# An encoder layer on one core: filter pieces every two and a half attention steps instead of three, and the scores' sum and maximum in one instruction

## The chip, the core and the metric

The kernel is written in Bass for one core of one Trainium2 chip. A core has five engines, each with its own in-order queue: TensorE (PE), VectorE (DVE), ScalarE (ACT), GpSimd (POOL) and SyncE (SP), which here only issues DMAs. They meet through semaphores. The metric is device microseconds of one execution.

## What is computed

One bidirectional encoder layer over a prompt of 1024 tokens and a sample of 512 tokens, 1024 channels wide. Three dilated window attentions (groups of 8 heads), two long convolutions (done as DFTs), gates, an output projection and two RMS norms. The part that the change touches is the attention, and a preparation of the convolution's filters that runs beside it. Cut to what matters, one attention group is:

```
logits = einsum(q, k) * hd ** -0.5 + bias
logits = where(valid, logits, -1e30)
m = max(logits, axis=-1)
p = exp(logits - m)
den = sum(p, axis=-1)
o = einsum(p, v) / den ;  lse = m + log(den)
```

The three groups are then mixed by a softmax over their `lse`.

## The kernel before, in words

**Stages.** First come normalisation and the convolution's input projection (to about 568 us), then attention (to about 1328 us), then the convolutions by DFT (to about 1930 us), then the gates, the branch products and the output.

**Attention steps.** Attention runs in 6 half groups `H` (4 heads each) of 24 steps: 144 steps `N` (`NSTEP`). A step is one pair of heads on one tile of 128 tokens. PE's loop over N does, in this order: in odd steps the scores of the next two steps (`score_pair`, L1423); the transposes of this step's probabilities (`turn`, L1436); the product with the values of the step before (`value`, L1451); and a share of the projections q, k and v of the next half group (`project`, L1290, through `PARTS`). The last half group has no next one. So from step 120 to step 137 each step has only two or three small parts of its own late value tiles (12 or 18 matmuls of 256 columns), and steps 138 to 143 have none.

For step N+1, DVE (`scored`) adds the bias to the scores out of PSUM (L2172) and takes the negated maximum (L2178). ACT's loop over N does `copy` (the transposed probabilities out of PSUM, L1774), `evacuate` (a projection, L1755), `prob` of step N+1 (two exponentials, each with a sum that is read out after it, L1766), `result` in odd steps (L1783, L1784), and then its share of a filter piece. A step's `turn` waits for its `prob`, and the next `prob` stands behind `copy` on ACT: this loop between PE and ACT is the shortest period that a step can have.

**Filter pieces.** 48 pieces (`NPIECE`) of the filters' taps are loaded (`load_piece`, L980), combined on DVE (`piece_first`, `piece_second`, L2192 to L2201), split into a high and a low fp16 half (`piece_hi` on ACT, L1795; `piece_low` on DVE, L2207; two of each per piece) and stored (`store_piece`, L988 and L990). `piece_at(slot, lag)` says in which slot a piece's parts stand: slot 13 + N is attention step N, and the parts of a piece stand 1, 2, 3 and 4 slots behind its start. There is one buffer `py` for the first half of a piece, so `piece_hi(p, 0)` waits until the first store of piece p-1 has landed:

```
if p >= 1:
    act.wait_ge(py_out, 16 * p)
```

**SP's queue** runs over the same slots: stores and the next load of the pieces, then, by their slot, four bulk loads for the DFT stage: `itab` (L1025), the first signal (L1003) and the two halves of the first filter slab (L1037). When all projections are done it loads the DFT tables and two more slabs (L1053, L1049, L1055, L1043).

Of the kernel before, what the change touches and what calls it, by code (L numbers as in the profile page):

```python
# [21 lines left out]
ALU = mybir.AluOpType  # L22
ACT = mybir.ActivationFunctionType
AX = mybir.AxisListType
F32, FP16, I32 = mybir.dt.float32, mybir.dt.float16, mybir.dt.int32

P = 128
# [15 lines left out]
NEG = -1e30  # L43
# [220 lines left out]
def build(nc, ins, cst, y_p, y_s):  # L264
# [9 lines left out]
    with ExitStack() as ctx:  # L274
# [5 lines left out]
        ps = ctx.enter_context(nc.psum_tensor("ps", [P, 8, BANK], F32))  # L280
# [83 lines left out]
        lg = [grid(2, 2 * P) for _ in range(2)]  # L364
        pr = [grid(2, 2 * P) for _ in range(2)]
# [4 lines left out]
        stat = [cols[:, 2 * HH * i:2 * HH * i + 2 * HH] for i in range(6)]  # L370
# [56 lines left out]
        def hg16(a, n):  # L427
# [23 lines left out]
        names = """ld_small ld_tabs ld_gain dve_steps ld_w0 ld_w1 w_amax w_all w_scale w_hi w_lo g_amax g_all  # L451
            root_seed g_scale rows_T cols_ok fcols_ok pads_ok n_sq n_mean n_root n_rstd n_scaled n_T n_evA n_evD
            hn_saved u_ready u_evac u_mid u_tap u_conv h_mm h_arg h_sin b_mm b_rows b_stored b_copied a_ready a_evac
            a_score a_biased a_max a_prob a_pT a_ptcopied a_ov a_oevac f_gen f_gen_used f_ge f_up f_pq f_maxed f_alled ld_bound ld_ke ld_ko ld_ftab16
            p_first p_hi p_lo f_r f_im f_y f_post
            ld_hx ld_ftab ld_itab g_cmb g_third g_sc g_exp m_mul b_maxed b_alled b_scaled b_hi b_lo h_hi h_lo m_acc o_sq o_root o_r o_y""".split()
        S = {n: sem(n) for n in names}
# [33 lines left out]
        STEPS = NT * 2  # L491
# [154 lines left out]
        NPIECE = len(PIECES)  # L646
        PRELUDE, PIECE0 = NQK + 1, 5
# [8 lines left out]
        def piece_part(p, z, h):  # L656

            words = py if z == 0 else px_half(p, 1)
            return words.bitcast(FP16)[:, 4 * FQ * h:4 * FQ * (h + 1)]

        def piece_at(slot, lag):

            n = slot - PIECE0 - lag
            return range(n // 3, n // 3 + 1) if n % 3 == 0 and 0 <= n < 3 * NPIECE else range(0)

        def spectra(i, p, h):

# [10 lines left out]
        def wait_ready(eng, u):  # L678
            eng.wait_ge(bank_ready[u[0]], u[1] + 1)
# [232 lines left out]
        def _(sp):  # L912
# [100 lines left out]
            for slot in range(PRELUDE + NSTEP):  # L1013
# [17 lines left out]
                for part_ in range(2):  # L1031
                    if slot == TAIL + 6 + 3 * part_:
# [3 lines left out]
                        c = slice(8 * FQ * part_, 8 * FQ * part_ + 8 * FQ)  # L1036
                        sp.dma_start(first_ke_words[:, c], ks_d[0, 0][:, c]).then_inc(S["ld_ke"], 16)  # L1037

            def load_ke(i):
                pieces_stored(PIECE_END[i])  # L1040
                if i >= 2:
                    wait_ready(sp, uk[i - 1][K0_UNITS - 1])
                sp.dma_start(ke_words, ks_d[i, 0]).then_inc(S["ld_ke"], 16)  # L1043

            def load_ko(i):
# [14 lines left out]
            for i in range(NI):  # L1060
                s, q, o = ITEMS[i]
# [6 lines left out]
                c0, nch = chans(i)  # L1068
# [28 lines left out]
        def _(pool):  # L1097
# [63 lines left out]
            def load_bias(H):  # L1161
                g, h0 = H // 2, HH * (H % 2)
                if H >= 2:
                    pool.wait_ge(S["a_biased"], STEPS * (H - 1))
                if g < 2:
                    pool.dma_start(bwt[H % 2], skewed(g, P - 1, P, h0, BW)).then_inc(ld_bias[H % 2], 16)
                else:
                    for seq in range(2):
                        pool.dma_start(b2t[H % 2][:, :, P * seq:P * seq + P],
                                       skewed(2, P - 1 + seq * (2 * P - 1), P, h0, P)).then_inc(ld_bias[H % 2], 16)  # L1170
# [5 lines left out]
            for N in range(NSTEP + 2):  # L1176
# [5 lines left out]
                if N >= 3 and N % 2 == 1:  # L1182
                    H, g, t, _ = unit(N - 2)
                    n = (N - 3) // 2
# [34 lines left out]
            for i in range(NI):  # L1219
# [6 lines left out]
                s, q, o = ITEMS[i]  # L1226
# [3 lines left out]
                if o == 1:  # L1230
# [6 lines left out]
                    c, nch = chans(i)  # L1237
# [47 lines left out]
        def _(pe):  # L1285
# [123 lines left out]
            def score_pair(n):  # L1409

                N = 2 * n
                H, g, t, _ = unit(N)
                if N % STEPS == 0:
                    pe.wait_ge(S["a_evac"], SEQ[H, NQK - 1] + 1)
                    if N == 0:
                        pe.wait_ge(S["pads_ok"], 15)
                k0, kw = windows(g, t)[:2]
                if N >= 2:
                    pe.wait_ge(S["a_biased"], N)
                for x in range(2):  # L1420
                    for h in range(2):
                        r = slice(HD * h, HD * h + HD)
                        mm = pe.matmul(ps[:, 2 + h, 2 * P * x:2 * P * x + kw], qt[H % 2][r, x, P * t:P * t + P],  # L1423
                                       kt[H % 2][r, x, k0:k0 + kw], start=True, stop=True)
                        if x == 1:
                            mm.then_inc(S["a_score"], 1)
# [201 lines left out]
            for t in range(NT):  # L1628
                pe.wait_ge(mt_lo, t + 1)
                for half in range(2):  # L1630
                    n = MT_O + 2 * t + half
# [10 lines left out]
        def _(act):  # L1642
# [60 lines left out]
            for c in range(3 * KD):  # L1703
                u, o = ub[c % 2], ut[c % 3]
# [6 lines left out]
                if c >= 3:  # L1711
                    act.wait_ge(uc_out[c % 3], 16 * (c // 3))
                act.activation(o, u[:, 1:1 + UC_W], ACT.Identity, scale=cols[:, CW + 3 * KD + c:CW + 3 * KD + c + 1],
                               bias=cols[:, CB + c:CB + c + 1]).then_inc(S["u_mid"], 1)
# [42 lines left out]
            def prob(N):  # L1757
                H, g, t, h = unit(N)
                kw = windows(g, t)[1]
                o = stat[N // 2 % 6]  # L1760
                act.wait_ge(S["a_max"], N + 1)
                if N >= 2:
                    act.wait_ge(S["a_pT"], N - 1)
                for x in range(2):
                    c = h + 2 * x
                    act.activation(pr[N % 2][:, x, 0:kw], lg[N % 2][:, x, 0:kw], ACT.Exp, bias=o[:, c:c + 1],  # L1766
                                   accum_out=o[:, c + HH:c + HH + 1]).then_inc(S["a_prob"], 1)

            def copy(N):
# [182 lines left out]
            for ns, n in enumerate(GATES):  # L1952
# [8 lines left out]
                x = ns % N_A  # L1961
# [17 lines left out]
            for t in range(NT):  # L1979
                if 4 <= t + 3 < NT:  # L1980
                    merged_hi(t + 3)
                for half in range(2):
                    n = MT_O + 2 * t + half
                    m_wait(act, n)
                    for x in range(2):
                        j = 2 * half + x
                        act.activation(osq[:, WC * j:WC * j + WC], ps[:, n % 8, WC * x:WC * x + WC], ACT.Square,  # L1987
                                       scale=o_descale[t // 4][:, j:j + 1], accum_out=ssq2[:, 4 * (t % 2) + j:4 * (t % 2) + j + 1]
# [5 lines left out]
        def _(dve):  # L1994
            steps = [0]

            def chain(op):

                op.then_inc(S["dve_steps"], 1)
                steps[0] += 1  # L2000
# [133 lines left out]
            for c in range(3 * KD):  # L2134
                u, o = ub[c % 2], ut[c % 3]
# [20 lines left out]
            def scored(N):  # L2156
                H, g, t, h = unit(N)
                _, kw, b0, _, edge = windows(g, t)
                l = lg[N % 2]
                c0, c1 = 0, kw  # L2160
                if edge is not None:
                    c0, c1 = (edge[1], kw) if edge[0] == 0 else (0, edge[0])
                if N % STEPS == 0:
                    dve.wait_ge(ld_bias[H % 2], 16 * (H // 2 + 1 if H < 4 else 4))
                dve.wait_ge(S["a_score"], N + 1)
                if N >= 2:
                    dve.wait_ge(S["a_prob"], 2 * N - 2)
                if edge is not None:
                    chain(dve.memset(l[:, :, edge[0]:edge[1]], NEG))
                    settle()  # L2170
                bias = (bwt if g < 2 else b2t)[H % 2][:, h:h + 3:2, b0 + c0:b0 + c1]
                dve.tensor_tensor(l[:, :, c0:c1], ps[:, 2 + N % 2, :].rearrange("p (x c) -> p x c", x=2)[:, :, c0:c1], bias,  # L2172
                                  ALU.add).then_inc(S["a_biased"], 1)
                dve.wait_ge(S["a_biased"], N + 1)
                n = N // 2
                if h == 0 and n >= 6:
                    dve.wait_ge(S["a_oevac"], n - 5)
                dve.tensor_reduce(stat[n % 6][:, h:h + 3:2], l[:, :, 0:kw], AX.X, ALU.max, negate=True  # L2178
                                  ).then_inc(S["a_max"], 1)

            def look_ahead(H, m):
                prepare(H, m, lambda b: w_power(dve, chain, settle, b), lambda b: w_low(dve, b), lambda b: w_max(dve, b))
# [263 lines left out]
            for t in range(NT):  # L2446
                o, w = ogt[:, t % 4], wts[t // 2 % 2]
# [91 lines left out]
            for ns, n in enumerate(GATES):  # L2539
                x = ns % N_A  # L2540
# [15 lines left out]
                if N_A <= ns < N_H:  # L2556
# [4 lines left out]
                    h = hg_tile(x)  # L2561
# [105 lines left out]
```

## Time and profile before

| | us |
|---|---|
| median of 3 runs | 2621.7 (2620.71 to 2631.27) |
| profiled execution | 2629.01 |
| its span | 2627.2 |
| PE / DVE / ACT / POOL busy | 2521.8 / 1601.2 / 944.4 / 477.1 |
| DMA | 341.26 MB, 130 GB/s on the mean |

PE is busy in 96% of the span. A busy PE can still be slow: the matmuls' ends are modelled, and the clock that it is granted has two levels, which a stretch shows as its mean granted clock (1.00 is 2.4 GHz, 0.50 is 1.2 GHz). Step numbers in this text come from counting the transposes of L1436 back from the last one at 1325.78 us, which is step 143.

### The profile page before, as it was taken

The page shows a single profiled execution, that of the slowest core. Times are in us where ns is not written, and L with a number is a line of the kernel's source. Part 1 is how long each engine was busy: PE and PEld are TensorE (multiplying, and loading weights), DVE is VectorE, ACT ScalarE, POOL GpSimd, SP SyncE. Part 2 cuts the span into 40 slices and gives each one's busy share as a digit, 9 for nine tenths or more (in the row PEclk, how much of TensorE's full clock was granted, in tenths as well). Part 3 has the DMA queues.
Part 4 walks back from the last instruction along what each step waited for, and adds up shares of the span by engine and source line. Part 5 has one row for each costly group of instructions (what it writes and reads, how often), then busy time and mean ns, then how long its engine had stood idle before and what let it go on. Part 6 is the DMA issues. An engine that isn't in the chain of part 4 may idle for free. (4 is left out here: it accounts for less than half of the span.)

```text
span 2627.2 us, 36180 instructions
## 1 busy us (share of the span) xinstructions
PE 2521.8 (96%) x14232; PEld 1542.7 (59%) x14232; DVE 1601.2 (61%) x2279; ACT 944.4 (36%) x1901; POOL 477.1 (18%) x462
## 2 busy tenths in 40 slices
PE   6999998999999999999799999999989999999997
PEld 4444343357676767676688888656434444444586
DVE  5746656635655656565669999776773245533543
ACT  5322212235544555555543334232541113211231
POOL 0105554400000000010034453423110000000000
PEclk9999999999999999999889999999989999999999
DMA  5824535422333434343654352535431021110132
GB/s 197 302 95 158 195 149 184 173 108 99 128 133 114 144 111 153 114 167 117 229 201 161 117 188 111 194 147 197 150 118 63 32 81 33 33 33 32 57 97 81
DMA packets 145264, 341.26 MB, mean 130 GB/s; under 512 B 8137, under 2 KB 102581, under 8 KB 138056
## 3 DMA queue, kind: packets, MB, share of 16 engines
q1 hardware_dynamic: 126312, 238.94, 26.6%
q0 software_dynamic: 18640, 93.72, 9.2%
q10 hardware_dynamic: 144, 6.29, 0.7%
q8 instruction: 114, 1.87, 0.3%
q14 instruction: 54, 0.44, 0.1%
HBM read 215.10 MB, written 130.12 MB: 131 GB/s over the span
## 5 line engine op out<-in xcount | busy, mean ns | idle before, releaser
L1290 PE MATMUL ps<-mem 128*128 128x512 f16 (+1 forms) x9312 | 1748.3, 348 | 21.1 <-ACT mem L1673 5.3
L1290 PEld LDWEIGHTS ps<-mem 128*128 128x128 f16 x9312 | 927.7, 102 | 811.1 <-issue 75.5
L849 ACT ACTIVATE mem<-mem 128x2048 f16<-128x2048 f32 (+1 forms) x56 | 108.6, 1940 | 386.0 <-DVE mem L867 385.8
L2172 DVE TENSOR_TENSOR mem<-ps,mem 128x512 f32<-128x512 f32 (+2 forms) x144 | 79.8, 554 | 239.5 <-PE ps L1423 238.8
L1774 ACT ACTIVATE mem<-ps 128x512 f32<-128x512 f32 (+1 forms) x144 | 72.1, 500 | 311.7 <-PE ps L1436 311.3
L837 POOL PARTITION_ALL_REDUCE mem<-mem x56 | 44.1, 789 | 757.9 <-DVE mem L830 731.7
L874 DVE SCALAR_TENSOR_TENSOR mem<-mem 128x2048 f16<-128x2048 f32 (+1 forms) x56 | 132.7, 2369 | 80.4 <-ACT mem L849 80.4
L1542 PE MATMUL ps<-mem 128*128 128x256 f32 x768 | 171.4, 380 | 0.6
L1477 PE MATMUL ps<-mem 128*128 128x256 f32 (+1 forms) x640 | 168.7, 422 | 0.0
L1542 PEld LDWEIGHTS ps<-mem 128*128 128x128 f32 x768 | 144.5, 190 | 24.1 <-issue 5.5
L2207 DVE TENSOR_TENSOR mem<-mem 128x1024 f16<-128x1024 f32 x96 | 117.1, 1220 | 51.4 <-ACT mem L1795 50.9
L1477 PEld LDWEIGHTS ps<-mem 128*128 128x128 f32 x640 | 120.4, 190 | 41.8 <-issue 28.7
L1190 POOL DMA_DIRECT2D s_og<-mem x72 | 39.4, 547 | 577.9 <-ACT mem L1784 563.5
L1873 ACT ACTIVATE mem<-ps 128x512 f32<-128x512 f32 x96 | 57.0, 597 | 233.0 <-PE ps L1542 233.0
L1486 PE MATMUL ps<-mem 128*128 128x256 f16 (+1 forms) x1032 | 139.5, 296 | 0.0
L1965 ACT ACTIVATE mem<-ps,mem 128x512 f32<-128x512 f32 x69 | 46.2, 683 | 243.5 <-PE ps L1290 238.9
L1766 ACT ACTIVATE mem<-mem 128x256 f32<-128x256 f32 (+1 forms) x288 | 129.5, 455 | 10.6 <-DVE mem L2178 10.3
L2272 DVE TENSOR_TENSOR mem<-ps,mem 128x1024 f32<-128x1024 f32 x112 | 129.4, 1211 | 6.4 <-ACT mem L1854 5.6
L2103 DVE SCALAR_TENSOR_TENSOR mem<-ps,mem 128x512 f32<-128x512 f32 x96 | 67.8, 742 | 100.8 <-PE ps L1374 69.8
L830 DVE TENSOR_REDUCE mem<-mem 128x1 f32<-128x2048 f32 (+1 forms) x56 | 123.2, 2202 | 4.1 <-DMA mem<-in_w_in 4.1
L1486 PEld LDWEIGHTS ps<-mem 128*128 128x128 f16 x1032 | 101.3, 98 | 36.5
L1451 PE MATMUL ps<-mem 128*128 128x64 f32 x896 | 119.2, 272 | 0.0
(191 smaller groups left out, 2597.0 us busy)
## 6 DMA issues: line engine op xcount, KB each, us to landing
s_ks<-mem SPq DMA_DIRECT2D x96, 512.0 KB, 2.7
mem<-s_ks SPq DMA_DIRECT2D x23, 2048.0 KB, 8.7
mem<-in_w_in SPq DMA_DIRECT2D x44, 1024.0 KB, 6.2
s_sums<-mem POOLq DMA_DIRECT2D x24, 1024.0 KB, 4.3
mem<-s_sums SPq DMA_DIRECT2D x48, 512.0 KB, 3.8
s_uc<-mem POOLq DMA_DIRECT2D x24, 768.5 KB, 6.1
mem<-s_uc SPq DMA_DIRECT2D x18, 1024.0 KB, 6.6
s_og<-mem POOLq DMA_DIRECT2D x72, 132.0 KB, 2.7
```

The lines of the kernel that those rows point to most:

```text
L830: dve.tensor_reduce(amax[b % 3], raw_of(b).rearrange("p k c -> p (k c)"), AX.X, ALU.max, apply_absolute_value=True).then_inc(S["w_amax"], 1)
L849: act.activation(w_place(b)[:, 0, 0:chunks(b)], raw_of(b), ACT.Copy, scale=wscale[b % 3]).then_inc(S["w_hi"], 1)
L874: dve.scalar_tensor_tensor(w[:, 1], raw_of(b), wscale[b % 3], w[:, 0], ALU.mult, ALU.subtract).then_inc(S["w_lo"], 1)
L1290: mm = pe.matmul(out, lhs(a, k), rhs(b, k), start=(k == 0 and x == 0), stop=(k == kc - 1 and x == 2))
L1451: mm = pe.matmul(ps[:, 6 + t % 2, c], pt[N % 2][:, x, P * b:P * b + P], vring[:, 2 * v_slot(H, vi // 2) + vi % 2, c], start=(b == 0), stop ...
L1477: mm = pe.matmul(out, ftab[:, P * n:P * n + P], a[:, comp, :], start=(x == 0), stop=(x == len(terms) - 1))
L1486: mm = pe.matmul(out, ftab16[:, a, n, :], slab[:, xs, z, b, j, :], start=(y == 0 and v == 0), stop=(y == len(terms) - 1 and v == 2))
L1542: mm = pe.matmul(ps[:, fbank(u), FQ * lane + oc:FQ * lane + oc + w], yf[:, 2 * p + b, FQ * im + c:FQ * im + c + P], itab[:, INVW * half + ...
L1766: act.activation(pr[N % 2][:, x, 0:kw], lg[N % 2][:, x, 0:kw], ACT.Exp, bias=o[:, c:c + 1], accum_out=o[:, c + HH:c + HH + 1]).then_inc(S[ ...
L2172: dve.tensor_tensor(l[:, :, c0:c1], ps[:, 2 + N % 2, :].rearrange("p (x c) -> p x c", x=2)[:, :, c0:c1], bias, ALU.add).then_inc(S["a_bias ...
L2207: dve.tensor_tensor(piece_part(p, z, 1), px_half(p, 1 - z), piece_part(p, z, 0), ALU.subtract).then_inc(S["p_lo"], 1)
L2272: op = dve.tensor_tensor(o.rearrange("p k a c -> p (k a) c"), z.unsqueeze(1).to_broadcast([P, 4, FQ]), k.rearrange("p k a c -> p (k a) c") ...
```

## The change

Pieces start at slot 5 + floor(5p/2) instead of 5 + 3p. The last part of the last piece stood in slot 150 (step 137) and now stands in slot 126 (step 113); the gaps between pieces are two and three slots in turn. DVE's two instructions for a step's scores become one `tensor_tensor_reduce` for each of the two heads. It writes the negated, biased scores and the minimum of those, and the exponential takes a scale of -1. The semaphore `a_biased` goes, and who waited for it (PE's next scores, POOL's bias load) waits for `a_max`. SP's second slab load waits for the first slab's halves.

```
+        PIECE_SLOT = [PIECE0 + 5 * p // 2 for p in range(NPIECE)]
+
         def piece_at(slot, lag):
 
-            n = slot - PIECE0 - lag
-            return range(n // 3, n // 3 + 1) if n % 3 == 0 and 0 <= n < 3 * NPIECE else range(0)
+            return [p for p in range(NPIECE) if PIECE_SLOT[p] + lag == slot]
...
                 if i >= 2:
                     wait_ready(sp, uk[i - 1][K0_UNITS - 1])
+                else:
+                    sp.wait_ge(S["ld_ke"], 32)
                 sp.dma_start(ke_words, ks_d[i, 0]).then_inc(S["ld_ke"], 16)
...
-                    pool.wait_ge(S["a_biased"], STEPS * (H - 1))
+                    pool.wait_ge(S["a_max"], STEPS * (H - 1))
...
-                    pe.wait_ge(S["a_biased"], N)
+                    pe.wait_ge(S["a_max"], N)
...
-                    act.activation(pr[N % 2][:, x, 0:kw], lg[N % 2][:, x, 0:kw], ACT.Exp, bias=o[:, c:c + 1],
+                    act.activation(pr[N % 2][:, x, 0:kw], lg[N % 2][:, x, 0:kw], ACT.Exp, scale=-1.0, bias=o[:, c:c + 1],
                                    accum_out=o[:, c + HH:c + HH + 1]).then_inc(S["a_prob"], 1)
...
-                    chain(dve.memset(l[:, :, edge[0]:edge[1]], NEG))
+                    chain(dve.memset(l[:, :, edge[0]:edge[1]], -NEG))
                     settle()
                 bias = (bwt if g < 2 else b2t)[H % 2][:, h:h + 3:2, b0 + c0:b0 + c1]
-                dve.tensor_tensor(l[:, :, c0:c1], ps[:, 2 + N % 2, :].rearrange("p (x c) -> p x c", x=2)[:, :, c0:c1], bias,
-                                  ALU.add).then_inc(S["a_biased"], 1)
-                dve.wait_ge(S["a_biased"], N + 1)
                 n = N // 2
                 if h == 0 and n >= 6:
                     dve.wait_ge(S["a_oevac"], n - 5)
-                dve.tensor_reduce(stat[n % 6][:, h:h + 3:2], l[:, :, 0:kw], AX.X, ALU.max, negate=True
-                                  ).then_inc(S["a_max"], 1)
+                for x in range(2):
+                    op = dve.tensor_tensor_reduce(l[:, x, c0:c1], ps[:, 2 + N % 2, 2 * P * x + c0:2 * P * x + c1], bias[:, x], -1.0, -NEG,
+                                                  ALU.add, ALU.min, stat[n % 6][:, h + 2 * x:h + 2 * x + 1])
+                    if x == 0:
+                        chain(op)
+                op.then_inc(S["a_max"], 1)
```

**ACT's order in steps 130 and 131.** First the kernel before, from the end of step 129; the line numbers are those above.

```order
L1795 ACTIVATE mem<-mem 128x1024 [waits py_out,p_first]
L1774 ACTIVATE mem<-ps 128x2x128 [waits a_ov,a_pT]
L1766 ACTIVATE mem<-mem 128x128 [waits a_pT,a_max]
L1766 ACTIVATE mem<-mem 128x128
L1795 ACTIVATE mem<-mem 128x1024 [waits p_lo]
L1774 ACTIVATE mem<-ps 128x2x128 [waits a_ov,a_pT]
L1755 ACTIVATE mem<-ps,mem 128x512 [waits a_ready]
L1766 ACTIVATE mem<-mem 128x128 [waits a_pT,a_max]
L1766 ACTIVATE mem<-mem 128x128
L1783 ACTIVATE mem<-mem 128x8 [waits a_prob,ot_out1,a_ov]
L1784 ACTIVATE mem<-ps 128x256
```

The same two steps in the changed kernel, whose lines stand three further down (`copy` is L1777, `prob` L1769, `result` L1786 and L1787).

```order
L1777 ACTIVATE mem<-ps 128x2x128 [waits a_ov,a_pT]
L1769 ACTIVATE mem<-mem 128x128 [waits a_pT,a_max]
L1769 ACTIVATE mem<-mem 128x128
L1777 ACTIVATE mem<-ps 128x2x128 [waits a_ov,a_pT]
L1758 ACTIVATE mem<-ps,mem 128x512 [waits a_ready]
L1769 ACTIVATE mem<-mem 128x128 [waits a_pT,a_max]
L1769 ACTIVATE mem<-mem 128x128
L1786 ACTIVATE mem<-mem 128x8 [waits a_prob,ot_out1,a_ov]
L1787 ACTIVATE mem<-ps 128x256
```

The two `piece_hi` are gone from here, with their waits for the store (`py_out`) and for DVE (`p_lo`); the rest is the same.

**SP's queue at the end of attention**, before (from the load of `itab`):

```order
L1025 DMA mem<-c_inv 128x3328 [waits a_ov]
L988 DMA s_ks<-mem 128x1024 [waits p_lo]
L990 DMA s_ks<-mem 128x1024 [waits p_lo]
L980 DMA mem<-s_sums 128x4x256 [waits px_out1]
L1003 DMA mem<-s_uc 128x2x1024 [waits uc_out1,uc_out2,uc_out0,a_ready]
L988 DMA s_ks<-mem 128x1024 [waits p_lo]
L990 DMA s_ks<-mem 128x1024 [waits p_lo]
L980 DMA mem<-s_sums 128x4x256 [waits px_out0]
L1037 DMA mem<-s_ks 128x2048 [waits px_out0,px_out1,py_out,w_lo]
```

And in the changed kernel, from the last piece's stores (L989, L991) to the second slab:

```order
L989 DMA s_ks<-mem 128x1024 [waits p_lo]
L991 DMA s_ks<-mem 128x1024 [waits p_lo]
L1026 DMA mem<-c_inv 128x3328 [waits a_ov]
L1004 DMA mem<-s_uc 128x2x1024 [waits uc_out1,uc_out2,uc_out0,a_ready]
L1038 DMA mem<-s_ks 128x2048 [waits px_out0,px_out1,py_out,w_lo]
L1038 DMA mem<-s_ks 128x2048
L1056 DMA mem<-c_fwd 128x7168 [waits hn_saved,a_ready]
L1052 DMA mem<-s_ks 128x4096 [waits px_out1,px_out0,py_out]
L1058 DMA mem<-c_fwd 128x3328
L1046 DMA mem<-s_ks 128x4096 [waits px_out1,ld_ke,px_out0,py_out]
```

No store of a piece stands between the four bulk loads any more, and nothing else does: they follow one another.

**DVE's order in two steps of the last half group**, before:

```order
L2172 TENSOR_TENSOR mem<-ps,mem 128x2x128 [waits a_prob,a_score]
L2178 TENSOR_REDUCE mem<-mem 128x2 [waits a_oevac,a_biased]
L2207 TENSOR_TENSOR mem<-mem 128x1024 [waits dve_steps,p_hi]
L2172 TENSOR_TENSOR mem<-ps,mem 128x2x128 [waits a_prob,a_score]
L2178 TENSOR_REDUCE mem<-mem 128x2 [waits a_biased]
L2207 TENSOR_TENSOR mem<-mem 128x1024 [waits dve_steps,p_hi]
L2192 TENSOR_TENSOR mem<-mem 128x512 [waits ld_piece1]
L2194 TENSOR_TENSOR mem<-mem 128x512 [waits dve_steps]
```

In the changed kernel:

```order
L2179 ISA mem<-ps,mem 128x128 [waits a_oevac,a_prob,a_score]
L2179 ISA mem 128x1
L2179 ISA mem<-ps,mem 128x128
L2179 ISA mem 128x1
L2179 ISA mem<-ps,mem 128x128 [waits a_prob,a_score]
L2179 ISA mem 128x1
```

A step's two instructions have become four: for each head one over the scores and one that writes its minimum (128x1). The pieces' instructions are gone from these steps, and stand in earlier ones.

## Rows read from the trace of the kernel before

**Rows 1.** Stretch, length, busy PE, PEld, DVE, ACT, POOL, clock, DMA share, GB/s

```profile
580.00:1240.00 660.00, 655.91 (x4528) 452.09 (x4527) 397.37 (x569) 343.79 (x883) 48.88 (x78) 1.00 0.37 128
1248.70:1315.40 66.70, 53.39 (x423) 46.02 (x422) 43.96 (x73) 38.46 (x125) 4.87 (x9) 0.85 0.69 234
1315.40:1328.80 13.40, 10.23 (x57) 8.93 (x56) 3.19 (x8) 8.30 (x35) 1.62 (x3) 0.63 0.93 347
```

**Rows 2.** Waits between 568 and 1190 us: waiter, releaser, total us, times, longest

```profile
ACT mem L1774 <- PE ps L1436: 269.9, 97, 4.9
...
DVE mem L2172 <- PE ps L1423: 203.3, 45, 6.8
```

**Rows 3.** The same view, 1248.7 to 1315.4 us

```profile
PE ps L1436 <- ACT mem L1766: 13.2, 8, 3.7
ACT mem L1795 <- DMA s_ks<-mem: 12.0, 4, 4.4
```

**Rows 4.** PE in order of time, steps 120 to 123: start, us, line

```profile
1248.74 0.38 PE L1436 MATMUL ps<-mem 128*128 128x128 f32 x2
...
1251.40 0.44 PE L1436 MATMUL ps<-mem 128*128 128x128 f32 x2
...
1253.38 0.41 PE L1436 MATMUL ps<-mem 128*128 128x128 f32 x2
...
1256.07 0.44 PE L1436 MATMUL ps<-mem 128*128 128x128 f32 x2
```

**Rows 5.** ACT and PE in order of time around one stall

```profile
1267.28 0.19 ACT L1766 ACTIVATION_READ_ACCUMULATOR mem<-mem 128x1 f32 x1
1271.15 1.06 ACT L1795 ACTIVATE mem<-mem 128x1024 f16<-128x1024 f32 x1 [3.68 <-DMA s_ks<-mem]
...
1273.30 0.69 PE L1436 MATMUL ps<-mem 128*128 128x128 f32 x2 [3.63 <-ACT mem L1766]
```

**Rows 6.** PE and its weight loads in order of time: steps 135, 136, 138, first DFT transposes

```profile
1302.46 0.49 PE L1436 MATMUL ps<-mem 128*128 128x128 f32 x2
...
1304.77 0.20 PEld L1436 LDWEIGHTS ps<-mem 128*128 128x128 f32 x2 [0.37 <-ACT mem L1766]
...
1315.39 0.63 PE L1436 MATMUL ps<-mem 128*128 128x128 f32 x2
...
1328.84 3.66 PE L1560 MATMUL ps<-mem 128*128 128x128 f32 x16 [0.77 <-ACT mem L1784]
```

**Rows 7.** DMAs of one line, issue to landing: a piece's first store, then attention's results

```profile
L988 SPq DMA_DIRECT2D s_ks<-mem x48: 319/320/465, 545.4 to 1310.5; - x48
...
DMA to landing us min/median/max: 2.6/2.6/10.5
...
L1190 POOL DMA_DIRECT2D s_og<-mem x72: 539/540/744, 596.2 to 1328.9; - x72
...
DMA to landing us min/median/max: 2.0/2.7/9.2
```

**Rows 8.** SP and ACT in order of time around one store in steady attention

```profile
980.37 0.32 SPq L988 DMA_DIRECT2D s_ks<-mem  x1
...
982.85 0.19 ACT L1766 ACTIVATION_READ_ACCUMULATOR mem<-mem 128x1 f32 x1
...
984.29 0.38 ACT L1774 ACTIVATE mem<-ps 128x256 f32<-128x256 f32 x1 [1.24 <-PE ps L1436]
```

**Rows 9.** DVE's groups by shape: count, busy us, mean ns, idle us before

```profile
L2178 DVE TENSOR_REDUCE mem<-mem 128x2 f32<-128x512 f32 x80 | 54.9, 686 | 2.8
L2172 DVE TENSOR_TENSOR mem<-ps,mem 128x512 f32<-128x512 f32 x64 | 44.0, 687 | 148.8 <-PE ps L1423 148.8
...
L2172 DVE TENSOR_TENSOR mem<-ps,mem 128x256 f32<-128x256 f32 x64 | 26.9, 420 | 90.0 <-PE ps L1423 90.0
...
L2634 DVE SCALAR_TENSOR_TENSOR mem<-ps,mem 128x256 f32<-128x256 f32 x48 | 21.0, 479 | 0.9
...
L867 DVE TENSOR_SCALAR mem<-mem 128x1 f32<-128x1 f32 x56 | 10.2, 182 | 0.0
```

More of the change, by code:

```diff
@@ L453, in build @@
             hn_saved u_ready u_evac u_mid u_tap u_conv h_mm h_arg h_sin b_mm b_rows b_stored b_copied a_ready a_evac
-            a_score a_biased a_max a_prob a_pT a_ptcopied a_ov a_oevac f_gen f_gen_used f_ge f_up f_pq f_maxed f_alled ld_bound ld_ke ld_ko ld_ftab16
+            a_score a_max a_prob a_pT a_ptcopied a_ov a_oevac f_gen f_gen_used f_ge f_up f_pq f_maxed f_alled ld_bound ld_ke ld_ko ld_ftab16
             p_first p_hi p_lo f_r f_im f_y f_post
```

## The prediction

> **What bounds the kernel now.** I read the busy time by stretches first, then who waits for whom inside the stretches that the change touches, then single steps in order of time. The page gives PE 96% of the span, so only two things can move the time: what PE computes, which the change leaves alone, and the places where PE idles or runs at the lower clock. In steady attention PE is busy 655.9 of 660 us at a granted clock of 1.00, with DVE at 397 and ACT at 344 [rows 1]. There ACT waits for PE's transposes 97 times, 2.8 us each on the mean, and DVE for PE's scores 45 times, 4.5 us each [rows 2]: both are ahead of PE.
>
> In steps 120 to 137 this turns round. The stretch is 66.7 us long, PE is busy 53.4, and the clock is 0.85 on the mean [rows 1]. PE's transposes wait 13.2 us for ACT's exponentials, and ACT in turn waits 12.0 us, in four waits, for the landing of a piece's store [rows 3]. One of these shows the chain: ACT ends the exponentials at 1267.47 and stands idle 3.68 us until `piece_hi` (L1795) may start. The next copy and exponentials stand behind it in ACT's queue, and PE idles 3.63 us before its next transposes. These then take 0.69 us instead of 0.44: the clock has gone from its upper level to the lower one behind the idle time [rows 5, 4].
>
> **The stores.** A first store lands in 2.6 us on the median, but in up to 10.5 [rows 7]. The long ones stand where SP has put a bulk load in front of them. The Trainium skill (DMA: Bandwidth & Descriptors, section Queues, rings and completion order) says that a semaphore's increment lands only after every earlier write of the same DMA engine; by that rule, the trace agrees.
>
> **What the change removes.** Pieces end at step 113 instead of 137. All 48 are still made; the ones that stood in steps 114 to 137 move to steps where PE is the bound. In steps 120 to 137 two `piece_hi` for every three steps leave ACT, and 5.2 us of piece work for every three steps leave DVE (two halves at 1.2 us and four instructions at 0.7).
>
> What is left there is PE's own work. I take it in two ways. PE's busy time scaled to the upper clock is 53.39 x 0.85 = 45.4 us [rows 1]. And an odd step that nothing stops takes 1.98 us from transpose to transpose (1251.40 to 1253.38), an even one 2.69 (to 1256.07, the next scores included) [rows 4]. That is 4.67 for a pair and 42.0 for nine pairs, to which the third projection parts of four steps come, 24 matmuls. The two agree, and I take 45.4.
>
> Does ACT keep up when the pieces are gone? Its loop from one transpose to the next is the transpose, the copy, two exponentials with their read-outs, and in some steps an evacuation. Step 135 shows that loop with an evacuation and without a piece: 2.31 us, of which the weight load that opens the transposes waited 0.37 [rows 6], so 0.33 more than PE's 1.98. Only two evacuations fall behind an odd step (131 and 135); those behind an even step have 2.69 us and fit. That is 0.7 us, and I add 0.4 for small waits: 45.4 + 0.7 + 0.4 = 46.5 us instead of 66.7, **20.2 us less**. The stretch of steps 138 to 143 has no projections and is bound by the loop between PE and ACT. No piece was in it, so it keeps its 13.4 us, of which I take off 0.3 for the faster start.
>
> **The denser pieces in steady attention.** In every second gap the next piece's `piece_hi(p, 0)` now comes one step after the store of the piece before, not two. I read the margin from 45 stores of the trace as the time between the store's landing (2.65 us behind its issue) and the end of the next step's exponentials on ACT. Among the 40 that stand before step 120 it is never negative; the smallest is the one shown: issue at 980.37, landing at 983.02, ACT free at 983.04, and another 1.25 us until ACT's next copy, which a `piece_hi` of 1.05 us fits into [rows 8]. So I cost this at 0. The cover is ACT's wait for PE, 2.8 us on the mean [rows 2]. DVE gets 5.2 us of pieces every 2.5 steps instead of every 3, which is 0.35 us a step on top of 3.1 in a step of 5.2 [rows 1]; it stays under PE.
>
> **The fused instruction.** The trace of before has none. By shape, DVE's two-tensor instructions take 420 ns for 256 columns and 687 for 512 [rows 9], so 267 ns for 256 columns more and, as an estimate, 286 ns for 128. For a step with 512 columns before stand 687 + 686 = 1.37 us. After, there are two instructions over 256 columns and two of 128x1. The lower bound is 2 x 0.42 = 0.84, with the small ones free; the upper one is 2 x (0.479 + 0.182) = 1.32, from the scalar form at 256 columns and a 128x1 instruction [rows 9]. That is less by 0.05 to 0.53 us on an engine that waits for PE: nothing. In the last half group the scores are 2 x 128 columns. Before it takes 0.42 + 0.42 and the gap between them, 0.88. After it is 2 x 0.286 = 0.57 at least and 2 x (0.345 + 0.182) = 1.05 at most, with the scalar form's surcharge of 59 ns. It is on PE's path only in odd steps, where the scores are one step old and the exponentials start as soon as DVE and the copy are done. Nine such steps give from -2.8 to +1.5 us, but below 0 nothing comes back, since PE's own 1.98 is then the bound. I take 0, nearest to the middle. The Trainium skill (VectorE: DVE Perf Modes, section Two Vector instructions with no wait between them) says that an operation that writes out its accumulator is two instructions, which the changed order shows. The Trainium skill (Vector Engine (DVE) Microarchitecture Reference, section Points that are easy to get wrong) also says that this layout with two 4-byte sources in SBUF runs at half rate; one source is in PSUM here, so whether it applies no row shows.
>
> **SP and POOL.** The four bulk loads now follow one another from about step 121. They are needed at the DFT stage or behind the end of the projections; nothing in between waits for them. SP's new wait for the slab's halves is passed some 40 us after they were issued: 0. `a_max` instead of `a_biased` lets PE's next scores go some 0.4 us later, but they stood behind a whole step already: 0.
>
> **The sum.** -20.2 - 0.3 = -20.5 us. The profiled execution goes from 2629.0 to 2608.5. It stands 7.3 us above the median of 2621.7, and the rows don't say where. If all of it lay in these stalls, the runs would gain 13.2; if none, 20.5. With 20.5 the median becomes 2601.2, and I lean a little to the first: **2602 us**. Its own range is 2596 to 2609.
>
> **Rivals.**
> *The fused instruction runs at half rate.* A step's two main instructions over 128 columns take 2 x (0.286 + 0.133) = 0.84 us and the two small ones up to 0.36, together 1.2 instead of 0.88. The exponentials of nine odd steps come 0.3 us later and PE pays 2.9, and steps 138 to 143 pay 0.9: the gain is 16.7, the time 2605. [...] Against it: the scalar form from PSUM and SBUF takes only 479 ns for 256 columns [rows 9]. Chance 0.14.
> *The bulk loads stop attention by another door.* Four loads in one block (4.7 MB) go out while the results' stores (L1190) run; a result waits for the store three results before it, some 13.5 us. At the 347 GB/s of steps 138 to 143 [rows 1] the block takes 14 us. Were a store held back that long, ACT would stand some us in `result`, once or twice, the clock would fall again, and half the gain would go: -10, so 2612. Against it: those stores never took more than 9.2 us [rows 7], although four went out under the block of loads after step 138. The rule of the Trainium skill on completions (DMA: Bandwidth & Descriptors) named above speaks for it. The same time comes out if the clock doesn't recover: 46.5 us of work at a clock of 0.85 is 54.7, a gain of 12. Chance 0.15.
> *DVE becomes the bound, slower.* In steady attention DVE has 3.13 us of work in a step of 5.2; with the denser pieces 3.48, of which 1.37 is the scores. If one fused instruction and its small one took 1.55 us together for 256 columns, DVE would reach 5.2; from there each 0.1 us costs 0.2 a step in some 80 steps, 16 us. At 1.7 us the gain is gone and the time is 2626, at 1.8 it is 2642. It decides at 1.68. Against it is the 479 ns row. Chance 0.05.
> *More than forecast*: the clock stays up through steps 138 to 143 and over the DFT stage's first transposes, whose 16 took 3.66 us [rows 6]. 3 to 6 us more: 2597. Chance 0.08. My forecast has 0.58.
>
> **How the numbers follow.** A measurement of this kernel tells about 0.5%, 13 us, from no change: below 2608.6 counts as faster. The forecast and the larger gain give 0.66, less 0.05 for the case that much of the 7.3 us lies in the stalls; half rate gives 0.14, nearly all below 2608.6; the third case is within 0.5% for the most part: faster 0.78, same 0.17, slower 0.05. The range for 8 in 10 leaves out DVE as the bound and the ends: 2594 to 2614.
>
> **What would show it.** Between the transposes of steps 120 and 138, 46 to 48 us instead of 66.7, at a clock of 0.95 or more, and no wait of L1795's successor for a store. The fused instruction under 0.5 us at 256 columns. In steady attention still over 99% of PE. The prediction is wrong if ACT waits for `py_out` in steady attention in more than a few steps, if the results' stores land in over 13 us, or if PE idles before the transposes of odd steps on DVE's minimum.

## The result, and the profile after

The changed kernel takes 2604.09 us on the median of 7 runs (2593.49 to 2610.14), the kernel before 2625.55 of 7, four more than stand in the table ahead of the prediction: a ratio of 0.9922 with a 95% interval of 0.9904 to 0.994. Two more comparisons of the same kernel, below, gave 0.9933 (0.9919 to 0.9948) and 0.9924 (0.99 to 0.9947). So it is faster by 0.7 to 0.8%. 2602 us was forecast, 19.7 under the 2621.7 known then; by the ratio it became 20.5. The profiled execution took 2607.87 us, with a span of 2606.1.

First the busy time of the changed kernel in steady attention, then in steps 120 to 137 and in steps 138 to 143; the columns are those of [rows 1].

```profile
580.00:1240.00 660.00, 657.19 (x4552) 454.54 (x4550) 367.49 (x838) 353.07 (x890) 50.50 (x77) 1.00 0.41 144
...
1251.60:1296.60 45.00, 44.78 (x422) 41.60 (x421) 8.40 (x72) 26.89 (x113) 4.65 (x9) 1.00 0.36 137
1296.60:1309.90 13.30, 9.96 (x58) 8.66 (x57) 1.95 (x16) 8.27 (x35) 1.84 (x4) 0.64 0.94 372
```

Against [rows 1], steps 120 to 137 have shrunk from 66.7 to 45.0 us. PE idles 0.2 us of them instead of 13.3, and the clock is 1.00 instead of 0.85. The last six steps are as they were.

The waits of the changed kernel in steps 120 to 137 answer to [rows 3]:

```profile
ACT mem L1777 <- PE ps L1439: 18.8, 18, 1.7
```

The direction has turned: ACT waits for PE in every one of the 18 steps, 1 us each, and no store is waited for.

The transposes (L1439) of steps 120 to 123 start at 1251.60, 1254.26, 1256.24 and 1258.90: 1.98 us for an odd step and 2.66 for an even one, as before where nothing stopped PE [rows 4]. DVE's groups by shape, which answer to [rows 9]:

```profile
L2179 DVE CUSTOM_DVE_ANT_0 mem<-ps,mem 128x256 f32<-128x256 f32 x128 | 49.0, 420 | 153.8 <-PE ps L1426 153.8
L2179 DVE CUSTOM_DVE_ANT_0 mem<-ps,mem 128x128 f32<-128x128 f32 x128 | 31.0, 286 | 118.0 <-PE ps L1426 117.6 <-ACT mem L1769 0.3
L2179 DVE DVE_READ_ACCUMULATOR2_ANT mem<- 128x1 f32 x288 | 23.8, 83 | 0.0
```

The main instruction takes at 256 columns what a plain addition of that shape takes, 420 ns [rows 9]; the one that writes the minimum takes 83.

**Where the time went.** The trace can be cut at four points that every kernel here has: the first scores, step 120's transposes, step 138's, and the DFT stage's first transposes. All lengths in us, one profiled execution each; the experiments are told below.

| kernel | to first scores | to 120 | to 138 | to DFT | to the end | span |
|---|---|---|---|---|---|---|
| before | 568.4 | 680.4 | 66.7 | 13.5 | 1298.4 | 2627.2 |
| changed | 572.8 | 678.8 | 45.0 | 13.3 | 1296.2 | 2606.1 |
| changed, second | 569.8 | 679.2 | 45.0 | 12.9 | 1296.7 | 2603.6 |
| changed, third | 566.1 | 678.8 | 45.0 | 13.0 | 1296.3 | 2599.1 |
| pieces' slots alone | 566.4 | 682.4 | 45.2 | 12.7 | 1297.5 | 2604.1 |
| the same, second | 563.0 | 685.1 | 45.2 | 12.8 | 1297.0 | 2603.0 |
| fused instruction alone | 567.5 | 677.1 | 61.9 | 12.3 | 1298.4 | 2617.2 |
| before, late bulk loads | 562.9 | 680.5 | 47.8 | 11.7 | 1306.9 | 2609.8 |
| a piece every two steps | 563.4 | 691.3 | 45.0 | 12.6 | 1297.6 | 2609.9 |
| fused doubled at the end | 573.3 | 679.8 | 46.7 | 12.9 | 1297.2 | 2609.9 |
| last projections over 20 steps | 573.9 | 678.7 | 41.8 | 13.6 | 1298.7 | 2606.7 |
| the same, tables first | 559.3 | 678.3 | 41.8 | 13.7 | 1299.2 | 2592.2 |

Up to step 120 six of the rows have the same code: the three of the changed kernel, the doubled one and the last two. Before the first scores they spread from 559.3 to 573.9 us, which is why single spans say little here. From there to step 120 the six lie between 678.3 and 679.8, and the two rows with the kernel before's code at 680.4 and 680.5. So the stretches say more than the totals.

There is only one profile of the kernel before, and it is a long one. Behind the first scores it is 25.1 to 25.8 us longer than the three of the changed kernel, where by their ratios the runs differ by 17.6 to 20.5. In every row of the table the difference behind the first scores is larger than the one of the runs, by 3.7 to 9.0 us. What follows takes differences against this profile, and some 6 us of it are not typical. They are probably in steps 120 to 138, since the stretches beside them repeat in other rows (680.5 and 1298.4) and the stretch came out at 61.9 with the fused instruction alone, where the stores and loads stand as before; no second profile of before shows it. If so, the 21.6 us there are nearer 16 in a typical execution.

### The profile page after: what moved, and what is told of

Read it like the earlier page. It is cut to its first block and busy times, and to the rows that moved or that the text cites. A ratio compares the mean times of both kernels' runs of the same rounds, so it can differ in the third digit from the quotient of the medians.

```text
span 2606.1 us, 36416 instructions
## 1 busy us (share of the span) xinstructions
PE 2511.2 (96%) x14232; PEld 1538.0 (59%) x14232; DVE 1537.9 (59%) x2567; ACT 943.0 (36%) x1901; POOL 481.9 (18%) x462
## 5 line engine op out<-in xcount | busy, mean ns | idle before, releaser
L2179 DVE CUSTOM_DVE_ANT_0 mem<-ps,mem 128x256 f32<-128x256 f32 (+2 forms) x288 | 90.2, 354 | 272.3 <-PE ps L1426 271.4
L1777 ACT ACTIVATE mem<-ps 128x512 f32<-128x512 f32 (+1 forms) x144 | 72.3, 502 | 313.6 <-PE ps L1439 313.2
L1545 PE MATMUL ps<-mem 128*128 128x256 f32 x768 | 171.5, 380 | 0.6 <-POOL mem L1206 0.2
L1545 PEld LDWEIGHTS ps<-mem 128*128 128x128 f32 x768 | 144.5, 190 | 24.2 <-issue 5.5
L1480 PEld LDWEIGHTS ps<-mem 128*128 128x128 f32 x640 | 120.4, 190 | 41.8 <-issue 28.7
L1769 ACT ACTIVATE mem<-mem 128x256 f32<-128x256 f32 (+1 forms) x288 | 129.3, 455 | 10.3 <-DVE mem L2179 10.2
```

What stands on the lines that cost most here:

```text
L1480: mm = pe.matmul(out, ftab[:, P * n:P * n + P], a[:, comp, :], start=(x == 0), stop=(x == len(terms) - 1))
L1545: mm = pe.matmul(ps[:, fbank(u), FQ * lane + oc:FQ * lane + oc + w], yf[:, 2 * p + b, FQ * im + c:FQ * im + c + P], itab[:, INVW * half + ...
L2179: op = dve.tensor_tensor_reduce(l[:, x, c0:c1], ps[:, 2 + N % 2, 2 * P * x + c0:2 * P * x + c1], bias[:, x], -1.0, -NEG, ALU.add, ALU.min, ...
```

## Experiments

**1. The pieces' slots alone.** The scores keep their addition and their maximum.

```
-            n = slot - PIECE0 - lag
-            return range(n // 3, n // 3 + 1) if n % 3 == 0 and 0 <= n < 3 * NPIECE else range(0)
+            return [p for p in range(NPIECE) if PIECE_SLOT[p] + lag == slot]
```

> Only the pieces' slots change (two and a half steps), the scores keep their two instructions. In the traces of before and of the changed kernel, steps 120 to 138 take 66.7 and 45.0 us, and the stretch from the first scores to step 120 takes 680.4 and 678.8 us. Theory (the pieces are the whole gain): 45 to 47 us for steps 120 to 138, time about 0.992 of before (0.990 to 0.994). Rival (the shorter score instructions do part of it): 49 us or more, and a ratio of 0.994 or more.

Measured: 2608.32 us on the median of 7 runs, 0.995 of before (0.9932 to 0.9968). Steps 120 to 138 take 45.2 us, as the theory has it, but the stretch before them grew to 682.4. So the moved pieces are the whole gain in the last half group, and the stretch before it is longer with them. The ratio of 0.995 lies outside the theory's 0.990 to 0.994 and on the rival's side, but the rival wanted 49 us or more in steps 120 to 138 as well.

**2. The fused instruction alone.** The changed kernel with pieces every three steps.

```
-        PIECE_SLOT = [PIECE0 + 5 * p // 2 for p in range(NPIECE)]
+        PIECE_SLOT = [PIECE0 + 3 * p for p in range(NPIECE)]
```

> Only the fused instruction, the pieces stay at every three steps. Theory: the four waits of ACT for a piece's first store stay (8 to 13 us), steps 120 to 138 take 60 to 68 us, time 0.999 to 1.001 of before. Rival (the fused instruction matters on its own): under 60 us for steps 120 to 138, or a ratio under 0.998.

Measured: 2620.46 us, 0.9989 of before (0.9972 to 1.0006). ACT's wait for a piece's store between step 120 and step 138:

```profile
ACT mem L1798 <- DMA s_ks<-mem: 9.7, 4, 4.8
```

The four waits for a store are still there, 9.7 us instead of 12.0, and steps 120 to 138 take 61.9 us. The theory holds for the stall. The 3.3 us less to step 120 were not in it.

PE's idle time accounts for most of them. From 580 us to step 120 PE waits 3.9 us before (3.9 too in the kernel of experiment 3), and 1.6 here. The five waits that are gone have one chain. DVE sets the scale of a weight tile (L867) behind a step's scores, ACT converts the tile (L849) when it has the scale, and the evacuation that PE waits for, or the exponentials behind it, stand behind that. Step 19 before, then with the fused instruction:

```profile
692.28 2.00 ACT L849 ACTIVATE mem<-mem 128x2048 f16<-128x2048 f32 x1 [0.82 <-DVE mem L867]
...
695.00 1.24 PE L1290 MATMUL ps<-mem 128*128 128x512 f16 x5 [0.74 <-ACT mem L1755]
```

```profile
690.30 2.00 ACT L850 ACTIVATE mem<-mem 128x2048 f16<-128x2048 f32 x1 [0.19 <-DVE mem L868]
```

The scale comes earlier, and PE goes on without a wait.

**3. The kernel before, with the bulk loads behind the last store.** Pieces and scores stay as they were, so ACT and DVE have the same work in these steps. The last lines of the edit, the wait of the second slab's load, are in the changed kernel too.

```
-            TAIL = PRELUDE + NSTEP - STEPS + 3
+            TAIL = 151
-                if slot == TAIL + 3:
+                if slot == TAIL + 1:
-                    if slot == TAIL + 6 + 3 * part_:
+                    if slot == TAIL + 2 + part_:
+                else:
+                    sp.wait_ge(S["ld_ke"], 32)
```

> The kernel before with its pieces and scores as they were; the four bulk loads (the inverse tables, the first signal, both halves of the first filter slab) are issued behind the last piece's stores instead of between them. Theory (it is the loads in front of the stores that stop ACT): ACT's waits for a piece's first store fall from 12.0 us to under 4, and steps 120 to 138 take 48 to 55 us instead of 66.7; how much of that is left in the time depends on how late the DFT stage's first loads then land, 0 to 15 us of it are lost there. Rival (the pieces' work on ACT and DVE is what is too much for steps this short): steps 120 to 138 still take 58 us or more.

Measured: 2616.54 us, 0.9975 of before (0.996 to 0.999). Busy time in steps 120 to 137, and ACT's two longest waits there:

```profile
1243.40:1291.20 47.80, 45.55 (x422) 41.53 (x421) 43.11 (x73) 38.41 (x125) 4.35 (x9) 1.00 0.58 211
```

```profile
ACT mem L1776 <- PE ps L1438: 5.0, 6, 1.4
ACT mem L1768 <- DVE mem L2180: 4.3, 5, 1.4
```

This decides between the two. DVE is busy 43.1 us and ACT 38.4, as in [rows 1], yet the stretch is 47.8 us at a clock of 1.00, and no store is waited for. Of the 21.6 us, measured against the one long profile of before, 18.8 come from the loads in front of the stores; the pieces' work in steps this short is worth the other 2.8. Part of what is won is lost again at the DFT stage, where PE's weight loads (L1488) now wait 8.0 us for the tables (`c_fwd`): to the end it takes 1306.9 us instead of 1298.4.

**4. A piece every two steps.** The changed kernel with `PIECE0 + 2 * p`.

> The changed kernel with a piece every two steps, so each piece's first store and the next load of its buffer have one step. A load can only go when the second store has landed: 2.6 + 0.5 + 3.8 us, against a step of 5.2. Theory (DVE's and ACT's lead over PE covers it): the first scores to step 120 within 3 us of 678.8, time within 0.2% of the changed kernel, with waits of DVE for loads of 20 us or more that PE does not see. Rival (the cover is used up): that stretch 5 us or more longer, with waits of PE for the exponentials behind it.

Measured: 2611.55 us, 0.9967 of before (0.9951 to 0.9982). The rival is right. The waits between the first scores and step 120:

```profile
DVE mem L2196 <- DMA mem<-s_sums: 52.0, 20, 5.9
...
PE ps L1293 <- ACT mem L1758: 6.4, 3, 3.1
...
PE ps L1426 <- ACT mem L1758: 4.6, 1, 4.6
...
ACT mem L1798 <- DMA s_ks<-mem: 3.1, 2, 1.7
```

DVE stands 52 us for the pieces' loads, and this time PE feels it: the stretch takes 691.3 us instead of 678.8. Followed back, five of PE's six waits there (in steps 50, 52, 54, 70 and 78) lead through DVE to such a load and from it to the second store in front; the sixth, 0.7 us in step 102, does not. So the first bound to give way is not the store that ACT waits for (3.1 us) but the next load behind the second store.

**5. The changed kernel and the pieces alone, side by side.**

> The changed kernel once more, beside the two below on one chip, to compare it with the pieces' part alone. Theory: 0.992 to 0.994 of before, 0.1 to 0.3% under the pieces alone, since in the traces the fused instruction takes 3.5 us from the stretch between the first scores and step 120 (682.4 to 678.8). Rival (that difference is chance): no difference to the pieces alone beyond 0.1%, and a stretch of 682 us or more.

> The pieces' slots alone, once more. Theory: 0.994 to 0.996 of before, and the stretch from the first scores to step 120 at 682 to 683 us, steps 120 to 138 at 45.2. Rival: a stretch that differs from the first run by more than 1.5 us, so that stretches can't be compared so finely.

Measured: the changed kernel 2606.45 us, 0.9933 (0.9919 to 0.9948); the pieces alone 2609.14 us, 0.9943 (0.9928 to 0.9957). The stretches to step 120 are 679.2 and 685.1 us. The order is the expected one, but the two intervals overlap, so the total alone doesn't show the fused instruction's part. In the traces it does: 677.1 to 679.8 us in the seven profiles with it at these cadences (without the one at two steps), 680.4 to 685.1 in the four without. PE's waits from 580 us to step 120 go the same way: 1.6 us for the fused instruction alone, 2.3 to 2.6 in the three of the changed kernel, 3.9 before, 5.5 and 6.6 with the pieces alone. The two profiles of the pieces alone differ by 2.7 us, more than I allowed.

**6. The fused instruction twice in the last half group.**

```
-                for x in range(2):
+                heads = (0, 0, 1, 1) if H == 5 else (0, 1)
+                for y, x in enumerate(heads):
+                    if y % 2 == 1 and H == 5:
+                        settle()
```

> The changed kernel with each fused instruction of the last half group issued twice, with a wait for the first between them: about 0.8 us more of DVE work in each of its 24 steps, nothing else. Theory (DVE's minimum is on PE's path in odd steps, with the copy on ACT just ahead of it, so everything beyond 0.9 us counts): steps 120 to 138 take 49 to 52 us instead of 45.0. Rival (it is hidden): under 46.5 us.

Measured in the trace: 46.7 us for steps 120 to 138, so neither the theory's 49 to 52 nor the rival's under 46.5, but next to the rival's limit; the total, 0.9944 (0.9922 to 0.9966) from two runs, says nothing on 1.6 us. An odd step of this kernel in order of time, from DVE's first instruction to its last minimum and what follows:

```profile
1260.84 0.29 DVE L2182 CUSTOM_DVE_ANT_0 mem<-ps,mem 128x128 f32<-128x128 f32 x1 [2.70 <-PE ps L1426]
...
1261.94 0.08 DVE L2182 DVE_READ_ACCUMULATOR2_ANT mem<- 128x1 f32 x1
1262.06 0.41 ACT L1769 ACTIVATE mem<-mem 128x128 f32<-128x128 f32 x1 [0.45 <-DVE mem L2182]
...
1262.99 0.20 PEld L1439 LDWEIGHTS ps<-mem 128*128 128x128 f32 x2 [0.34 <-ACT mem L1769]
```

DVE is on PE's path here, as argued, but the sizes are smaller. One step's scores take 1.2 us doubled (1260.84 to 1262.02) where the undoubled one takes 0.5, so 0.7 more, of which 0.34 reaches PE's weight load in this step and 0.18 on the mean of nine pairs.

**7. The last projections over 20 steps.** With no pieces there, nothing but the projections' own due times sets their spread.

```
-        AHEAD = 6
+        AHEAD = 4
```

> The changed kernel with the last half group's projections spread over 20 steps instead of 18, two parts in each. Theory (with no pieces there, a step with two parts takes PE's own 4.67 us for a pair, and only steps without parts are bound by the loop between PE and ACT, some 2.1 us each): from step 120 to the DFT stage 55.5 to 57 us instead of 58.3. Rival (evacuations and value products now come too late, or the tables' loads, issued later, hold up the DFT stage): 58 us or more, or over 1 us added behind the DFT stage's start.

Measured: 2607.71 us, 0.9935 (0.9921 to 0.9949), beside 0.9933 of the changed kernel on the same chip. From step 120 to the DFT stage it is 55.4 us instead of 57.9 to 58.3, as expected. The rest of the trace gives it back. A wait of PE for a table appears in the DFT stage (0.4 us, under `filter_dft`), and to the end it takes 1298.7 us.

**8. The tables first.** The same, and the second item's slab waits until the signal tables have landed.

```
             sp.dma_start(ftab, cst["fwd"]).then_inc(S["ld_ftab"], 16)
+            sp.wait_ge(S["ld_ftab"], 16)
```

> The kernel with the last projections over 20 steps, and with the load of the second item's filter slab held back until the signal tables have landed. In the run without it, PE waited 0.4 us for those tables in the DFT stage, and that stage took 1298.7 us to the end against 1296.2 to 1296.7 in two profiles of the changed kernel. Theory (the slab takes bandwidth from the tables, and the tables' landing costs the 2 us): no wait of PE for the tables, DFT stage to the end 1296 to 1297.3 us, from step 120 to the DFT stage 55 to 56 us. Rival (those 2 us are chance, or the slab is now late itself): 1298 us or more, or a wait for the slab.

> The changed kernel beside it. Theory: 0.992 to 0.994 of before; stretches 679, 45.0 and 13 us and 1296 to 1297 to the end. The kernel above should stand 0.1% under it if its stretches add up.

Measured: 2598.38 us, 0.9923 (0.9895 to 0.995), and the changed kernel 2601.46, 0.9924 (0.99 to 0.9947). No difference can be told. The theory fell: PE still waits for a table before the same instructions, now 0.9 us. The tables are issued when the last projection is done, and this spread puts that 8.8 and 8.9 us ahead of the DFT stage instead of 13.1 (changed kernel). From the DFT stage's first transposes to its first inverse product (L1545) these two kernels take 29.7 and 30.1 us, the changed one 28.7, 29.2 and 29.1. That is up to 1 us of the 2 to 3 that they are longer. The rest lies behind the last inverse product. There, from the start of that product on, the twelve profiles spread over 2 us, and I see no order by edit in it: 793.1 to 793.4 us in before, the fused instruction alone, the doubled one and these two, 792.0 and 792.2 in the piece every two steps and the late bulk loads, 791.3 to 791.9 in the three of the changed kernel and the two of the pieces alone. What sets it I did not find out.

## Why the prediction was right, and where its terms were off

**The stall.** The step "ACT waits for a store, the next exponentials stand behind it, PE idles and the clock falls" is shown by experiment 3, which takes the loads away from the stores and leaves the pieces and the scores: no wait for a store, the clock at 1.00, 18.8 us less. The Trainium skill (DMA: Bandwidth & Descriptors, section Queues, rings and completion order) has a completion land only behind earlier writes of the same DMA engine; that the loads in front are the cause agrees with it, but no run here tells it apart from plain sharing of the bandwidth. It isn't SP's queue alone: before, attention's results, small stores on POOL's own queue, landed in 6.7 to 9.2 us in the five cases in steps 120 to 137 where they went out within 6 us behind a bulk load, and in 2.0 to 2.8 in the four with no bulk load under way.

**The term for steps 120 to 137.** Forecast 46.5 us, measured 45.0 to 45.2 in six profiles, just under the 46 to 48 named as the sign. PE's own work was right to 0.4 us. Its scaled busy time gave 45.4; the step times, which the prediction didn't add up, give 44.9: 42.0 for nine pairs, and 24 matmuls of which 12 take 1.47 us. The 1.1 us that I added for evacuations and small waits are almost all hidden: PE's weight loads wait 0.7 us in two steps. The 0.3 us taken off the last six steps are 0.2 to 0.5, which is within what these profiles spread.

**The denser pieces, costed at 0.** Here the step was wrong in size. The margin that I read, between a store's landing and ACT, did hold: ACT waits for a store 0.2 us in all in the pieces alone, and not at all in the changed kernel. But I never priced the other chain, second store, next load, `piece_first` on DVE. DVE waits 13.0 us for pieces' loads between the first scores and step 120 of the changed kernel, and none before step 120 in the kernel before. Two waits of PE are new or longer in that profile, 0.4 us in step 97 and 1.2 in step 102. Both lead back to a second store that went out just behind a weight load of 1 MB: the main finding once more. The first of them, steps 93 to 97:

```profile
1119.39 0.43 SPq L825 DMA_DIRECT2D mem<-in_w_in  x1
1120.83 0.70 SPq L991 DMA_DIRECT2D s_ks<-mem  x1
...
1129.77 0.54 SPq L981 DMA_DIRECT2D mem<-s_sums  x1
...
1134.08 0.69 DVE L2196 TENSOR_TENSOR mem<-mem 128x512 f32<-128x512 f32 x1 [3.59 <-DMA mem<-s_sums]
...
1142.03 0.44 PE L1439 MATMUL ps<-mem 128*128 128x128 f32 x2 [0.39 <-ACT mem L1769]
```

The second store lands after 8.9 us instead of 2.7 on the median, the load goes out at once behind it, and DVE, late from then on, holds up the exponentials of step 97. Such waits of PE stand in steps 94 to 102 alone. A step takes 5.6 us on the mean (676.3 over 120, from transposes to transposes), not the 5.2 that I reckoned with, but from step 96 to step 119 it takes 5.0, the least of the five half groups.

With the scores as before, the denser pieces cost 2.0 and 4.7 us to step 120 (682.4 and 685.1 against 680.4), of which PE's waits show 1.6 and 2.7. With the fused instruction they cost 1.2 to 2.7 (678.3 to 679.8 in the six profiles against 677.1). Experiment 4 shows where that leads.

**The fused instruction, costed at 0.** Its price lies at the cheap end of my bounds, and under it in effect. The main instruction takes 420 ns at 256 columns and 286 at 128, the lower bounds. The 83 ns of the small one don't even count: the next main instruction starts 0.21 us after the one before at 128 columns (changed kernel, step 121, in order of time).

```profile
1254.58 0.28 DVE L2179 CUSTOM_DVE_ANT_0 mem<-ps,mem 128x128 f32<-128x128 f32 x1
...
1254.79 0.29 DVE L2179 CUSTOM_DVE_ANT_0 mem<-ps,mem 128x128 f32<-128x128 f32 x1
```

It is not nothing in steady attention, as I had it. "An engine that waits for PE" holds for DVE on the mean and not in the steps where a weight tile's scale stands behind the scores (experiment 2). The profiles with it are 3.3 us shorter to step 120 at three steps a piece, and 2.5 to 6.8 at two and a half.

**The sum.** The forecast was -20.5 us, and that the runs moved by 20.5 (15.8 to 25.2) is partly luck. In the profiles the term for steps 120 to 137 is -21.6 and was forecast at -20.2. Beside it stand -1.2 to -1.6 to step 120, two errors of opposite sign, and -1.7 to -2.2 behind the DFT stage's start, for which I had no term and found no cause. That makes 25.1 to 25.8 in all, and the long profile of before takes some 6 off again.

**The odd steps.** That DVE's minimum is level with the copy on ACT held before the change, with 0.88 us for a step's scores: in step 121 of the kernel before, ACT is done with the copy 0.15 us before the minimum is there. After it they take 0.5, and experiment 6 shows that 0.7 us more then costs PE only 0.18 a pair. The bounds of -2.8 to +1.5 us were far too wide for what is on the path.

**The rivals.** Half rate: the 420 ns row speaks against it, for one source in PSUM and one in SBUF; no run has both in SBUF. The bulk loads in one block: they went out at 1252.41 to 1253.83 us, and attention's results under them landed in 6.3 us at most, in 7.4 over the whole run, against 9.2 before [rows 7]; no `result` waited for a store. DVE as the bound: DVE's busy time in 660 us of steady attention fell from 397 to 367, although the pieces stand denser. A larger gain by the clock: steps 138 to 143 run at 0.64, against 0.63 before.

**From the trace to the median.** I left open whether the 7.3 us between the profiled execution and the median lay in the stall. Against the median of 7 runs they are 3.5. With all 7.3 in the stall the runs would have gained 13.2; the interval of the ratio begins at 15.8, so not all of it did. But the table shows the profile of before to be long behind the first scores, not in front of them, where its 568.4 us lie in the middle of 559.3 to 573.9. So part of it may well have lain in the stall, and the runs gained in the other stretches what they missed there.

## What to carry to other kernels

A small store whose landing an engine waits for should not stand behind bulk loads. Another queue alone is not shown to help: the results on POOL's queue were late behind them too. Where the loads can't move, as here, where later ones made the next stage late, take the small traffic out of that stretch, even into steps where it costs a little. Mind every bulk load there, the weights' as well. And when work is packed denser, walk every chain of its buffers, the reload behind the second store as well as the one wait that is plain to see: that other chain was the first to give way. Last, an engine that idles 40% of the time is not off the path in every step: look for the steps in which another engine waits for something small behind its long work.

## What the runs showed that I had not expected

A two-source instruction with a running minimum, one source in PSUM, runs on DVE at the rate of a plain addition (420 ns for 256 columns of 4 bytes; 286 for 128, where no plain addition stands beside it), and reading out its minimum adds nothing that can be seen. The time to the first scores spreads over 15 us between profiles of the same code, which is most of what single runs differ by. The stretch behind the last inverse product runs from 791.3 to 793.4 us, for a cause that stays open. And steps 120 to 138 with the four waits took 66.7 us in one profile and 61.9 in the other, with the fused instruction; whether that is the instruction or chance no run tells, and one trace of a stall is a weak measure of its size.
